# Summing the weighed modulation tiles over partitions: block transposes and column sums on VectorE, one TensorE matmul per block

## The reference

```python
shift, scale, gate = jnp.split(jax.nn.silu(c) @ w_mod + b_mod, 3, axis=-1)
shift_c, scale_c, gate_c = jnp.split(jax.nn.silu(c_ctx) @ w_mod + b_mod, 3, axis=-1)
...
hx = rmsnorm(x, g_pre) * (1 + scale[:, None]) + shift[:, None]
hc = rmsnorm(ctx, g_pre) * (1 + scale_c) + shift_c
...
x_new = x + gate[:, None] * rmsnorm(y, g_post)
```

## Time and profile before

| | |
|---|---|
| median of 3 runs | 1957.68 us (1957.17 to 1959.28) |
| span of the profiled execution | 1955.8 us |
| TensorE busy (matmul / weight load) | 1925.2 us (98%) / 1633.5 us (84%) |
| VectorE, ScalarE, GpSimd busy | 807.3, 829.7, 704.9 us |
| granted TensorE clock, mean | 0.998 |

### The profile page before, as it was taken

The page is one execution under the profiler, slowest core; times in us unless marked ns, Lnnn a source line. Parts: engine busy times, 40 slices in busy tenths (PEclk is TensorE's granted clock), DMA queues, the critical chain, the costliest instruction groups (busy, mean ns, idle before and its releaser), DMA issues.

```text
span 1955.8 us, 26905 instructions
## 1 busy us (share of the span) xinstructions
PE 1925.2 (98%) x10454; PEld 1633.5 (84%) x10454; DVE 807.3 (41%) x1827; ACT 829.7 (42%) x1582; POOL 704.9 (36%) x553
## 2 busy tenths in 40 slices
PE   8999999999999999999999999999999999999997
PEld 4898889878889888888888888888888898888886
DVE  3665557543556445576511110027367551111003
ACT  3321268365237556686232322115478432323222
POOL 0523312125440344311444445445321344444442
PEclk9999999999999999999999999999999999999999
DMA  9544311022340124211333333323420223333321
GB/s 282 163 163 162 119 65 45 19 57 87 108 146 6 57 68 131 88 55 44 87 86 105 89 108 108 108 78 95 122 81 23 66 77 105 99 94 100 128 88 44
DMA packets 198261, 183.72 MB, mean 94 GB/s; under 512 B 31702, under 2 KB 166220, under 8 KB 198136
## 3 DMA queue, kind: packets, MB, share of 16 engines
q1 hardware_dynamic: 192104, 170.67, 28.6%
q10 hardware_dynamic: 6032, 11.33, 1.9%
HBM read 179.86 MB, written 5.40 MB: 95 GB/s over the span
## 4 chain that ended last, share of the span: by engine, by line
PE 90%; ACT 3%; DVE 3%; issue 2%; POOL 2%; DMA 0%; SPq 0%; ACTq 0%; DVEq 0%
PE ps L1341 24%; PE ps L1343 24%; PE ps L1342 24%; PE ps L1938 3%; PE ps L1434 3%; PE ps L1855 3%; PE ps L1401 2%; POOL w_lo L733 2%; PE ps L1956 2%; PE ps L1420 2%; PE ps L1464 1%; ACT w_hi L788 1%; PE ps L1379 1%; PE ps L1362 1%; PE ps L1658 0%
## 5 line engine op out<-in xcount | busy, mean ns | idle before, releaser
L733 POOL TENSOR_TENSOR w_lo<-raw,w_hi 128x512 fp32r<-128x512 f32 (+1 forms) x518 | 679.9, 1343 | 1152.4 <-ACT w_hi L788 1152.3
L788 ACT ACTIVATE w_hi<-raw 128x1024 fp32r<-128x1024 f32 (+2 forms) x261 | 258.5, 1036 | 251.5 <-PE ps L1343 190.8
L1341 PE MATMUL ps<-g_hi,w_lo 128*128 128x512 f32 (+1 forms) x928 | 348.4, 375 | 1.4 <-POOL w_lo L733 1.4
L1342 PE MATMUL ps<-g_lo,w_hi 128*128 128x512 f32 (+1 forms) x928 | 347.5, 374 | 0.0
L1343 PE MATMUL ps<-g_hi,w_hi 128*128 128x512 f32 (+1 forms) x928 | 347.5, 374 | 0.0
L1341 PEld LDWEIGHTS ps<-g_hi,w_lo 128*128 128x128 f32 x928 | 174.7, 188 | 33.7 <-issue 1.7
L1343 PEld LDWEIGHTS ps<-g_hi,w_hi 128*128 128x128 f32 x928 | 174.7, 188 | 31.4
L1342 PEld LDWEIGHTS ps<-g_lo,w_hi 128*128 128x128 f32 x928 | 174.7, 188 | 30.9
L2659 DVE TENSOR_TENSOR tmp_f<-ps,tmp_f 128x512 f32<-128x512 f32 x44 | 30.4, 691 | 370.7 <-PE ps L1343 370.7
L1341 PE MATMUL ps<-h_hi,w_lo 128*128 128x512 f32 (+1 forms) x496 | 180.2, 363 | 3.3 <-DVE h_lo L2076 2.3
L1343 PE MATMUL ps<-h_hi,w_hi 128*128 128x512 f32 (+1 forms) x496 | 174.6, 352 | 0.0
(11 more groups left out here) (292 smaller groups left out, 3472.6 us busy)
## 6 DMA issues: line engine op xcount, KB each, us to landing
raw<-in_w_in SPq DMA_DIRECT2D x30, 1024.0 KB, 5.3
raw<-in_w_mod SPq DMA_DIRECT2D x24, 1024.0 KB, 6.1
raw<-in_w_gate SPq DMA_DIRECT2D x44, 512.0 KB, 4.0
raw<-in_w_up SPq DMA_DIRECT2D x44, 512.0 KB, 5.2
raw<-in_w_down SPq DMA_DIRECT2D x22, 1024.0 KB, 4.8
raw<-in_w_out SPq DMA_DIRECT2D x8, 1024.0 KB, 5.0
strips<-bias_rows ACTq DMA_DIRECT2D x18, 256.0 KB, 3.2
raw<-in_w_in SPq DMA_DIRECT2D x16, 256.0 KB, 4.5
```

Source lines behind the costliest of these rows:

```text
L733: pool.tensor_tensor(w_lo[:, i % SPLIT, a:e], raw_of(what)[:, a:e], w_hi[:, i % SPLIT, a:e].bitcast(F32), ALU.subtract).then_inc(s_tile_lo ...
L788: act.activation(w_hi[:, i % SPLIT, a:b], raw_of(what)[:, a:b], ACT.Copy).then_inc(s_tile_hi.sem, s_tile_hi.nth((what, n)))
L1341: pe.matmul(o, lhs[1], rhs[0], start=first, stop=False)
L1342: pe.matmul(o, lhs[0], rhs[1], start=False, stop=False)
```

## The change

VectorE takes over most of the sum over partitions. After the second `weigh` of a block it transposes each `acc` in blocks of 32 x 32 (two instructions, 128 x 512 each) into the slot of `raw` that the block's second tile came in, and then sums the 32 columns of each transposed block (two instructions, 128 x 512 to 128 x 16 each) into a new small buffer `row_sums`. After that each partition holds sums over one quarter of the partitions. TensorE adds the four quarters with one float32 matmul of 32 columns, whose weights are a new constant `quarters`, the 32 x 32 identity repeated 4 x 4. `summed_in` reads the 32 columns with four instructions of 32 partitions in place of one of 128.

With it go these edits: `quarters` is one more load among the constants, ahead of W0; `add_up` waits for the constants as well; the first `weigh` of block n no longer waits for `add_up` of block n - 2 but for VectorE's own work, and the wait for `add_up(n - 2)` stands ahead of the transposes, where it guards `row_sums`; and the block's second tile counts as used only when its column sums are done, since they read its slot.

```diff
+    c["quarters"] = np.tile(np.eye(32, dtype=f), (4, 4))
...
+        quarters = at("quarters", [P, P], free_at)
+        row_sums = [at(f"row_sums{i}", [P, 2, 16], free_at + 4 * P + 4 * 32 * i) for i in range(2)]
...
-        consts = [(rot[:], I["rot"]),
+        consts = [(rot[:], I["rot"]), (quarters[:], I["quarters"]),
...
             def add_up(n, b):
 
                 pe.wait_ge(s_weigh.sem, s_weigh.at(WEIGHED[2 * n + 1]))
-                for h in range(2):
-                    for c in range(4):
-                        o = 256 + 2 * c + h
-                        m = pe.matmul(ps[:, b, o:o + 1], acc[n % 2][h][:, P * c:P * c + P], ones[:, 0:1], start=True, stop=True)
+                pe.wait_ge(s_consts.sem, 16 * len(consts))
+                m = pe.matmul(ps[:, b, 256:288], quarters[:], row_sums[n % 2][:].rearrange("p h m -> p (h m)"), start=True, stop=True)
...
                 if kh == 0 and n >= 2:
-                    dve.wait_ge(s_mod.sem, s_mod.at(("sum", n - 2)))
+                    dve.wait_ge(s_weigh.sem, s_weigh.at(WEIGHED[2 * n - 3]))
...
+                if kh == 1:
+                    turned = raw_of(what)
+                    if n >= 2:
+                        dve.wait_ge(s_mod.sem, s_mod.at(("sum", n - 2)))
+                    for h in range(2):
+                        dve.wait_ge(s_weigh.sem, s_weigh.at((what, 3, h)))
+                        V.transpose(turned[:, 512 * h:512 * h + 512], acc[n % 2][h][:]).then_inc(s_weigh.sem, s_weigh.nth((what, "turned", h)))
+                    for h in range(2):
+                        dve.wait_ge(s_weigh.sem, s_weigh.at((what, "turned", h)))
+                        V.tensor_reduce(row_sums[n % 2][:, h, :], turned[:, 512 * h:512 * h + 512].rearrange("p (m i) -> p m i", i=32),
+                                        AX_X, ALU.add).then_inc(s_weigh.sem, s_weigh.nth((what, "summed", h)))
                 s_weigh.name_latest(what)
...
-                V.tensor_tensor(mod[:, :, 4 * jb:4 * jb + 4], ps[:, sum_bank(n), 256:264].rearrange("p (c s) -> p s c", s=2),
-                                vec_t[:, VB[wl]["b_mod"] + 4 * jb:VB[wl]["b_mod"] + 4 * jb + 4].unsqueeze(1).broadcast_to((P, 2, 4)),
-                                ALU.add).then_inc(s_mod_in.sem, s_mod_in.nth(("sum", n)))
+                for q in range(4):
+                    at_q = slice(32 * q, 32 * q + 32)
+                    V.tensor_tensor(mod[at_q, :, 4 * jb:4 * jb + 4],
+                                    ps[at_q, sum_bank(n), 256:288].rearrange("p (s c q) -> p q s c", s=2, q=4)[:, q, :, :],
+                                    vec_t[at_q, VB[wl]["b_mod"] + 4 * jb:VB[wl]["b_mod"] + 4 * jb + 4].unsqueeze(1).broadcast_to((32, 2, 4)),
+                                    ALU.add).then_inc(s_mod_in.sem, s_mod_in.nth(("sum", n)))
```

More of the change, by code:

```diff
@@ L277, in _program @@
         junk = at("junk", [P, D], uf_at)
+        free_at = -(-max(o + n for o, n in names.values()) // 32) * 32
+        quarters = at("quarters", [P, P], free_at)
+        row_sums = [at(f"row_sums{i}", [P, 2, 16], free_at + 4 * P + 4 * 32 * i) for i in range(2)]
         ps = ctx.enter_context(nc.psum_tensor("ps", [P, 8, 512], F32))
```

## The result

The changed kernel took 1963.32 us (median of 8 runs), the kernel before 1957.62 on the same chip (median of 8). One run of each took many times as long (9726 and 11064 us) and is left out of the ranges, 1961.87 to 1963.67 and 1957.17 to 1959.28, and of the ratio. The ratio is 1.0025, with a 95% interval of 1.0015 to 1.0035: slower by 0.25%, 5.7 us, where 6.6 us less had been forecast. The profiled execution has a span of 1961.9 us.

The account below looks back on a forecast made before the run. TensorE, busy for 98% of the span, was taken to bound the kernel. Layer 0 -8.9 us, layer 1 +2.3 and 0, together -6.6 us, took the median from 1957.7 to 1951.1 us, range 1946.5 to 1955.5.

Parts of the forecast that it names:

- What bounds the kernel: Whole kernel: TensorE's matmuls are busy for 98% of the span, so its time counts if what feeds it keeps up.
- TensorE's part: `add_up` on TensorE: 1.70 us becomes 0.21, a gain of 1.49 us a block, 11.9 us for eight.
- Rival 4: `add_up`: the new matmul costs 0.5 us, or its waits show, 1952.9 us; sum not shortened at all: chance 0.05.
- VectorE's part, the price: After each block's second `weigh`: four new VectorE instructions at 0.70 us each lengthen its queue by 2.5 us.
- d: Delay from VectorE's new instructions after a block's second `weigh`: 2.5 us, bounds 1.9 and 6.8.
- The wide bound: VectorE's four new instructions a block: all beside GpSimd at 1.78 us each, a delay of 6.8 us.
- Rival 2: VectorE's transposes are slower than a plain pass: at 1.24 us each the time is 1953.2 us; chance 0.20.
- rival 1: Ring slots: the later release costs nothing and all eight blocks gain, 1945.8 us; chance 0.10.
- Layer 1: Late slots in layer 1: zc's half tile ends 2.3 us later, ga0's block gains about nothing; +2.3 us together.
- the six blocks of layer 0 give their whole 1.49: Layer 0: no delay reaches TensorE, so six blocks save 1.49 us each, -8.9 us.
- the slot: Ring slot of a block's second tile: given back 2.5 us later; in layer 0 tightest at bc, 2.8 us left.
- Rival 3: Slots of W13, W15, then W5: VectorE's new work becomes the bound, slower from d above 5.7 us; chance 0.08.

Follow-up runs that it names:

- e5: Changed kernel with block 4's sum read before `weigh(11)`, transposes into `acc` with the slot given back before them, and layer 1's `weigh(13)` one step earlier: 1946.20 us.
- e3: Changed kernel with the transposes written into the other pair of `acc` and the ring's slot given back before them: 1954.78 us, ratio 0.9984.
- e6: Kernel before with one float32 matmul of 32 columns in place of the eight, and no transposes or column sums: 1947.38 us, ratio 0.9950.
- e8: Changed kernel with GpSimd waiting for `weigh(11)` before it makes ga1's low pieces: 1960.52 us, ratio 1.0010.
- e7: Kernel before with `quarters`, transposes and column sums added but their results unused, the eight matmuls and `summed_in` kept: 1962.57 us, ratio 1.0022.
- e2: Kernel before with `summed_in(4)` moved ahead of `weigh(11)` in layer 0: 1958.17 us, ratio 1.0000.
- e1: Changed kernel with `summed_in(4)` moved ahead of `weigh(11)` in layer 0: 1952.16 us, ratio 0.9969.

## Why the prediction was wrong

- **What bounds the kernel**: right. TensorE's time counted, and every version that kept it fed got its savings back (e5 all of them).
- **TensorE's part**: right. 0.15 us against 0.21; the gain is 1.55 us a block against 1.49. Rival 4, that it would not be shortened, falls.
- **VectorE's part, the price**: right. Transposes 0.68, column sums 0.65 us against 0.70 each, d = 2.4 against 2.5. No row stood behind the lower bound of 0.4 for a transpose. The wide bound, four at 1.78 beside GpSimd, was never met: none of the 32 instructions took over 0.70 us, though only five of them ran while GpSimd worked (the four of block 0 and the last sum of block 3). Rival 2 falls, and so does rival 1: zc's load was issued 2.4 us late.
- **Layer 1**: right in the cause, the late release (e3), and near in size (+2.5 against +2.3), the size in part by luck. TensorE waited for ScalarE's `v` and not for GpSimd's fourth piece; the 1.5 us of lower clock behind the wait were not in the sum; zc cost 2.9 instead of 2.3 us, and ga0 gained 0.8 instead of nothing.
- **Layer 0: "the six blocks of layer 0 give their whole 1.49"**: this step failed. It looked at one thing that the delay moves, the slot, and found bc's the tightest with 2.8 us to spare. No load was late enough for TensorE there. What was missed is one line up, in VectorE's part: `summed_in` and its reads "under the same waits for TensorE as `weigh` ... All these I cost at nothing". The read of a sum also gives back the bank that holds it. Its slack of 3.7 us could be read off the trace before, 224.15 - 220.46, and the two moves of the forecast's own numbers against it, about five savings of 1.5 us on one side and d on the other, come to 7.5 + 2.5 = 10, far more than 3.7. (That the measured wait is 10.0 us too is chance: 10 less the slack is 6.3, and the stretched `weigh(11)`, 6.2 us less the 2.0 by which VectorE was ahead otherwise, made up the rest.) Not all of that would have been lost, as e6 shows: with an earlier VectorE the read comes earlier too. But it would have been named as the tightest place of layer 0.
- **The size of that step**: 12 us, 10.0 of wait and 1.9 of slower matmuls behind it. A good 4 us of the wait came from `weigh(11)` beside GpSimd (e8), which the forecast had only as a cost of the new instructions and not of the old ones that shift.
- **Rival 3**, slower, had the sign and the wrong mechanism. It wanted d above 5.7 us at the slots of W13, W15 and W5; with d = 2.4 the kernel is slower all the same. Its chance of 0.08 was that of a price. No chance stood for a second resource that VectorE gives back.
- The forecast said that TensorE would be 8.9 us ahead at 450 us and 6.6 after 560: it was behind by 2.6 and 5.1 us, from the bank's wait on.

**What stays open.** The kernels with the new work on VectorE take 0.3 to 0.6 us more from `k_lo` of layer 1 to the end (1.2 in e7), where nothing is changed; and the time before `rr` differs by up to 4 us between the profiled executions. Neither was followed.

## What to carry to other kernels

List for each instruction that is delayed all that it gives back, PSUM banks and its engine's place in the queue too, and take the slack of each: for a bank, from the last read to the next group's first matmul. Where one engine gets ahead and another behind by the same change, the two shifts add up at such a place, and a slack that each alone would just about keep is gone. An early read of a small result, ahead of a long step in the same queue, cost nothing here (e2) and was worth 12 us of a stage (e1).

## What the runs showed of the hardware

- **A block transpose of float32 and a sum over groups of 32 columns** take VectorE 0.68 and 0.65 us for 128 x 512, as much as a plain pass of that size (0.74 for `weigh`).
- **Beside GpSimd** these were never longer, while `weigh`'s instructions, 8 in 5.38 us beside nothing, took 11.53 us for 8, six of them beside GpSimd's subtractions. The Trainium skill, page "SBUF — State Buffer", section "Who interferes with whom", says that a VectorE instruction with two SBUF inputs contends with a GpSimd one that reads SBUF, and that one with at most one SBUF input (outside the 2-port modes) does not. The trace agrees on both: `weigh` has `raw` and `acc` as inputs and is stretched to more than twice its time (up to 1.78 us for one), the transposes (659 to 698 ns) and column sums (632 to 667 ns) have one input and keep theirs, the five of the 32 beside GpSimd among them; in e3 nine stand beside it, and none of its 32 is over 0.71 us. By this rule the upper bound of d, 6.8 us, would have been 2.8, four at 0.70. It wasn't VectorE that gave way every time: in block 0 of the changed kernel GpSimd's first piece starts at 71.10 amid the products of `weigh(1)`, which keep their 0.73 us while the piece takes 4.57 instead of 1.29 us, until 1.2 us after the last of them.
- **A wait can cost more than itself.** After 10 us without work the same 128 x 256 matmuls took 0.213 instead of 0.12 us each for 4 us. The 24 matmuls behind the wait took 4.73 us after 10.0 us of waiting (the changed kernel), 5.04 us after 5.3 (e8), 4.27 us after 3.7 (e3) and 2.98 us after 0.48 (e6), against 2.87 with no wait. In these four the price doesn't follow the length of the wait.
